# Differential attention of the sample group with the keys along the partitions

## The reference

```python
def diff_attend(q, k, v, q_pos, k_pos, lam, rel_bias):
    s = jnp.einsum('bigrmd,bjgmd->bgrmij', q, k).astype(f32) * (HEAD_DIM ** -0.5)
    dist = q_pos[:, None] - k_pos[None, :]
    bias = rel_bias[rel_bucket(dist)]...            # (tq, tk, 4, 3), the same for both maps
    s = jnp.where(dist >= 0, s + bias, -jnp.inf)
    p = jax.nn.softmax(s, axis=-1)
    a = p[:, :, :, 0] - lam * p[:, :, :, 1]         # the two maps, subtracted
    return jnp.einsum('bgrij,bjgd->bigrd', a, v)    # v has 128 columns
```

## Time and profile before

| | us |
|---|---|
| median of 3 runs | 2465.31 (2454.02 to 2467.85) |
| profiled execution, whole | 2461.47 |
| its span, first to last instruction | 2459.7 |
| PE busy, share of the span | 2230.9 (91%) |
| DVE busy | 1233.1 (50%) |
| ACT busy | 1020.2 (41%) |
| mean granted PE clock | 0.921 |

### The profile page before, as it was taken

The page is one execution under the profiler, slowest core; times in us unless marked ns, Lnnn a source line. Parts: engine busy times, 40 slices in busy tenths (PEclk is TensorE's granted clock), DMA queues, the critical chain, the costliest instruction groups (busy, mean ns, idle before and its releaser), DMA issues. The chain is left out here.

```text
span 2459.7 us, 38651 instructions
## 1 busy us (share of the span) xinstructions
PE 2230.9 (91%) x15123; PEld 1980.8 (81%) x15123; DVE 1233.1 (50%) x2108; ACT 1020.2 (41%) x1569; POOL 416.1 (17%) x396
## 2 busy tenths in 40 slices
PE   6899979999866998999877799699998999979999
PEld 4888869999865456999865466499998888869999
DVE  5666645554442234554446433355546566655554
ACT  3666654443341113443354211444434656644442
POOL 2111102431000002341000000024311111102430
PEclk9899979999986797999985699899999899979999
DMA  5244525658620442657630546056577244436554
GB/s 170 86 134 142 159 70 155 172 156 268 209 76 12 112 125 85 170 160 223 211 103 20 180 139 205 34 162 172 156 238 220 78 142 142 136 94 170 159 154 137
DMA packets 505099, 352.45 MB, mean 143 GB/s; under 512 B 13548, under 2 KB 486398, under 8 KB 504218
## 3 DMA queue, kind: packets, MB, share of 16 engines
q1 hardware_dynamic: 503906, 323.01, 45.3%
q10 hardware_dynamic: 1024, 27.13, 2.8%
HBM read 326.59 MB, written 50.63 MB: 153 GB/s over the span
## 5 line engine op out<-in xcount | busy, mean ns | idle before, releaser
L249 PE MATMUL ps<-xh,wh 128*128 128x288 f32 x2368 | 652.8, 303 | 16.4 <-ACT wh L213 16.2
L221 DVE TENSOR_TENSOR wl<-raw,wh 128x2048 fp32r<-128x2048 f32 (+3 forms) x241 | 501.4, 2082 | 283.7 <-ACT wh L213 282.2
L249 PE MATMUL ps<-xl,wh 128*128 128x288 f32 x2368 | 643.5, 298 | 0.0
L213 ACT ACTIVATE wh<-raw 128x2048 fp32r<-128x2048 f32 (+3 forms) x241 | 419.0, 1741 | 309.9 <-PE ps L257 193.8
L249 PEld LDWEIGHTS ps<-xh,wh 128*128 128x128 f32 x2368 | 452.8, 191 | 18.4 <-issue 14.2
L249 PEld LDWEIGHTS ps<-xl,wh 128*128 128x128 f32 x2368 | 452.4, 191 | 0.5
L257 PE MATMUL ps<-xh,wl 128*128 128x288 f32 x2368 | 353.3, 300 | 0.0
L257 PEld LDWEIGHTS ps<-xh,wl 128*128 128x128 f32 x2368 | 327.0, 190 | 2.3
L473 POOL TENSOR_TENSOR gh<-sg,ut 128x288 f32<-128x288 f32 x88 | 216.6, 2462 | 351.6 <-ACT sg L411 351.6
L249 PE MATMUL ps<-hh,wh 128*128 128x288 f32 x704 | 194.5, 300 | 12.9 <-issue 12.5
L249 PE MATMUL ps<-hl,wh 128*128 128x288 f32 x704 | 193.3, 300 | 0.0
(11 more groups left out here) (317 smaller groups left out, 3113.9 us busy)
## 6 DMA issues: line engine op xcount, KB each, us to landing
raw<-in_ffn_w_in SPq DMA_DIRECT2D x176, 512.0 KB, 5.1
raw<-in_ssm_w_in SPq DMA_DIRECT2D x80, 512.0 KB, 4.9
raw<-in_ffn_w_out SPq DMA_DIRECT2D x64, 384.0 KB, 5.1
raw<-in_ffn_w_out SPq DMA_DIRECT2D x64, 320.0 KB, 3.4
H<-in_state_ssm SPq DMA_DIRECT2D x32, 512.0 KB, 7.4
out_ssm_sample<-H SPq DMA_DIRECT2D x32, 512.0 KB, 6.3
raw<-in_ssm_w_out SPq DMA_DIRECT2D x32, 512.0 KB, 5.3
Kp<-in_cache_diff_k SPq DMA_DIRECT2D x64, 256.0 KB, 4.1
```

Source lines behind the costliest of these rows:

```text
L213: act.activation(wts["hi"][:, s, 0:width], raw[:, s, 0:width], ACT.Copy).then_inc(hi_ready.sem, 1)
L221: dve.tensor_tensor(wts["lo"][:, s, 0:width], raw[:, s, 0:width], wts["hi"][:, s, 0:width].bitcast(F32), ALU.subtract).then_inc(lo_ready.s ...
L249: pe.matmul(out, W[0][:, kk, j, :], x_[:, k, :], stop=False, start=(part == 0 and kk == 0 and x_ is seg.hi), skip_group_check=True)
```

## The change

The sample phase is written anew. Keys now lie along the partitions of the scores:

- `scores` has the turned keys stationary (eight blocks of 128 x 128 per head group) and the 24 queries of the head group moving, and one more matmul for the new tokens. A batch's scores are nine blocks of 96 columns in banks 4 and 5.
- The bias is made in the same shape: 32 matmuls with 33 x 128 blocks of `oh` stationary and `rb` (12 columns) moving, and 4 for the new tokens; 16 DVE copies spread it over the two maps.
- The maximum of a score column now runs over partitions: DVE reduces the nine blocks (`column_max`), PE turns the result (`turn_max`), DVE reduces and puts it on a diagonal (`turn_back`), PE spreads it with a matmul by ones (`spread_max`), DVE subtracts (`shift`), ACT takes the exponential, DVE sums the blocks (`column_sum`), PE spreads the sum (`spread_sum`).
- `values` has the values stationary (128 x 128) and the 24 columns of unnormalised probabilities of both maps moving. DVE divides by the sum, multiplies by lambda and adds the maps into `OT`. There is no turning of probabilities or output, and no copy to `PT`.
- The loops over batches are written out on every engine, and POOL's copy of the queries is gone. SP's loads are as before, with the same two events to wait for.

PE's order in one batch: keys 0, `turn_max` of b-1, keys 1, scores 0, `spread_max` of b-1, keys 2, scores 1, keys 3, scores 2, scores 3, `spread_sum` of b-1, values of b-1.

```diff
             @block.tensor
             def _(pe):
...
-                    for half in range(2):
-                        pe.matmul(ps[32 * g:32 * g + 32, 4 + half, :], Qst[:, r, g, :],
-                                  KT[:, g, half * 512:half * 512 + 512], start=True, stop=True,
-                                  tile_position=(0, 32 * g))
...
+                    for j in range(NPAGES):
+                        bank, o = place(j)
+                        o += 24 * g
+                        pe.matmul(ps[:, bank, o:o + 24], KT[:, g, j * P:(j + 1) * P], Qall[:, b, g, :],
+                                  start=True, stop=True, skip_group_check=True)
+                    o = 288 + 24 * g
+                    mm = pe.matmul(ps[0:NS, 5, o:o + 24], X[:, QD_C + g, SEQ:TOK], Qall[:, b, g, :],
+                                   start=True, stop=True, skip_group_check=True)
...
+                def turn_max(b):
+                    pe.wait_ge(col_max.sem, col_max.at(b + 1))
+                    if b >= 1:
+                        pe.wait_ge(inverted.sem, inverted.at(b))
+                    pe.transpose(ps[0:96, 6, 0:P], cmax[:, b % 2, :], ident).then_inc(max_turned.sem, max_turned.inc())
+
+                def spread_max(b):
+                    pe.wait_ge(max_diag.sem, max_diag.at(b + 1))
+                    pe.matmul(ps[:, 6, P:P + 96], ones[0:96, :], dmax[:, b % 2, :], start=True, stop=True).then_inc(
+                        max_spread.sem, max_spread.inc())
+
+                def spread_sum(b):
+                    pe.wait_ge(col_sum.sem, col_sum.at(b + 1))
+                    pe.matmul(ps[:, 6, P + 96:P + 192], ones, csum[:, b % 2, :], start=True, stop=True).then_inc(
+                        sum_spread.sem, sum_spread.inc())
...
-                            v = Vp[:, r, n, g * P:(g + 1) * P] if n < NPAGES else KV[0:NS, 2, 1, g * P:(g + 1) * P]
-
-                            k, o = (P if n < NPAGES else NS), W * n + g * REP * T
-                            mm = pe.matmul(ps[32 * g:32 * g + 32, 7, 0:P], PT[0:k, r, o:o + 32], v,
-                                           start=(n == 0), stop=(n == NPAGES), tile_position=(0, 32 * g))
...
+                        out, c = ps[:, 7, 24 * g:24 * g + 24], slice(24 * g, 24 * g + 24)
+                        for j in range(NPAGES):
+                            pe.matmul(out, Vp[:, r, j, g * P:(g + 1) * P], Pe[:, j, c],
+                                      start=(j == 0), stop=False, skip_group_check=True)
+                        mm = pe.matmul(out, KV[0:NS, 2, 1, g * P:(g + 1) * P], Pe[0:NS, NPAGES, c],
+                                       start=False, stop=True, skip_group_check=True)
...
+                for j in range(NPAGES):
+                    for t in range(T):
+                        o = NH * (T * j + t)
+                        pe.matmul(ps[:, 4, o:o + NH], oh[:, t, j * P:(j + 1) * P], rb[:, :],
+                                  start=True, stop=True, skip_group_check=True)
...
+                for b in range(NB + 1):
+                    if b < NB:
+                        turn_keys(b, 0)
+                    if b >= 1:
+                        turn_max(b - 1)
+                    if b < NB:
+                        turn_keys(b, 1)
+                        scores(b, 0)
+                    if b >= 1:
+                        spread_max(b - 1)
+                    if b < NB:
+                        turn_keys(b, 2)
+                        scores(b, 1)
+                        turn_keys(b, 3)
+                        scores(b, 2)
+                        scores(b, 3)
+                    if b >= 1:
+                        spread_sum(b - 1)
+                        values(b - 1)
...
             @block.scalar
             def _(act):
...
+                for b in range(NB + 1):
+                    if b < NB:
+                        for g in range(3):
+                            keys(b, g)
+                    if b >= 1:
+                        exps(b - 1)
+                    if b < NB:
+                        keys(b, 3)
...
             @block.vector
             def _(dve):
...
+                for b in range(NB + 1):
+                    if b < NB:
+                        keys(b, 0)
+                    if b >= 1:
+                        turn_back(b - 1)
+                    if b < NB:
+                        keys(b, 1)
+                    if b >= 1:
+                        shift(b - 1)
+                    if b < NB:
+                        keys(b, 2)
+                        keys(b, 3)
+                    if b >= 1:
+                        column_sum(b - 1)
+                    if b < NB:
+                        add_bias(b)
+                        column_max(b)
+                    if b >= 1:
+                        out(b - 1)
```

More of the change, by code:

```diff
@@ L2442, in _ @@
             def _(pool):
[L2443 to L2453, removed]
+                pool.memset(Qall[:, :, :, :], 0.0).then_inc(filled.sem, filled.inc())
@@ L2455, in _, with place @@
+                pool.memset(Sb[:, :, NPAGES, :], NEG).then_inc(filled.sem, filled.inc())
+            def place(j):
+                return (4, 96 * j) if j < 5 else (5, 96 * (j - 5))
             @block.tensor
             def _(pe):
[L2457 to L2462, removed]
@@ L2502, in turn_out @@
-                def turn_out(b, r):
-                    pe.wait_ge(out_staged.sem, out_staged.at(b + 1))
-                    pe.transpose(ps[:, 7, P:2 * P], OS[:, r, :], ident).then_inc(out_turned.sem, out_turned.inc())
[L2506 to L2510, removed]
-                    turn_keys(b, r, 1)
-                    pe.wait_ge(q_staged.sem, q_staged.at(b + 1))
-                    pe.wait_ge(sc_ready.sem, sc_ready.at(3 * b))
-                    scores(b, r, 0)
-                    turn_keys(b, r, 2)
-                    scores(b, r, 1)
-                    if back:
-                        turn_probs(b - 1, 1 - r)
-                    turn_keys(b, r, 3)
-                    scores(b, r, 2)
-                    scores(b, r, 3)
-                    pe.wait_ge(pt_moved.sem, pt_moved.at(2 * b))
-                    for g in range(KVH):
-                        mm = pe.matmul(ps[32 * g:32 * g + 32, 6, NEWC:NEWC + NS], Qst[:, r, g, :],
-                                       X[:, QD_C + g, SEQ:TOK], start=True, stop=True, tile_position=(0, 32 * g))
-                    mm.then_inc(old_scored.sem, old_scored.inc())
-                    if back:
-                        values(b - 1, 1 - r, half - (1 - r))
@@ new lines, in _ @@
+                pe.wait_ge(row_set.sem, row_set.at(1))
+                pe.wait_ge(loaded.sem, loaded.at(2))
+                pe.wait_ge(new_laid.sem, new_laid.at(1))
+                for j in range(NPAGES):
[3 more added lines that the diff above has]
+                                  start=True, stop=True, skip_group_check=True)
+                for t in range(T):
+                    mm = pe.matmul(ps[0:NS, 5, NH * t:NH * t + NH], ohn[:, t, :], rb[:, :],
+                                   start=True, stop=True, skip_group_check=True)
```

292 lines of the change are left out of this document (146 added, 146 removed).

## The result

The changed kernel took 2553.64 us (median of 4 runs, 2546.91 to 2555.73) against 2459.66 for the kernel before in the same job (4 runs, 2454.01 to 2467.85): a ratio of 1.0364, with a 95% interval of 1.0317 to 1.0411, and a difference of 94.0 us. The profiled execution took 2546.91 us, 85.4 more than the profiled one of before.

A forecast was written before the change was run, and what follows sets the result against it. The stage was taken as TensorE's alone: 8 x 30.2 + 2 x 8.7 + 5 + 0.9 = 265 us, less 175.5 and 2.4, gives +87 on 2465.3, 2552 us. Range 2530 to 2585.

The forecast's parts named there:

- points 1, 2 and 4: TensorE per full-clock batch: scores 7.2 us against 7.0, values 8.6 against 8.8, together 20.9 (20.4 to 21.7) against 20.42.
- The draw: By instruction times alone the change neither gains nor loses: 20.9 us a batch against 20.42.
- The clock: Narrow matmuls lower TensorE's clock, transposes raise it: per batch 3.8 us low, 9.9 full, 16.5 low, together 30.2.
- A missed batch: A batch whose transposes miss the clock's rise stays low throughout: 38.9 us.
- How many batches miss: Two of eight batches let miss the clock's rise, 8.7 us for each.
- rival C: Mixed scores and transposes lose the full clock, or more batches miss: +105 to +125 us, about 2580; chance 0.16.
- point 5: VectorE's reductions, 1.0 us each in 9 us of work, hide under TensorE's batch of at least 20: cost nothing.
- point 6: Preparation: bias matmuls 14.7 us against 15.5, key transposes no longer wait for table copies; keys start 2.4 us earlier (0 to 4).
- point 7: Last batch's softmax steps follow each other while TensorE waits: 5 us (4 to 6), then values and 0.9 us of scaling.
- Rival A: Gapless narrow matmuls hold the full clock through the stage: -5 us (-8 to +5), 2460 us; chance 0.12.
- Rival B: The clock never comes back within the stage: +139 us, 2604 us; chance 0.04.

The follow-up runs named there:

- wide72_inorder: Changed kernel in its own order, tail and loads, every score and value matmul 72 columns wide for 24, scores laid out group by group: 2480.42 us, stage 223.3.
- after_again: The changed kernel itself, unedited, run again in the other job on another chip: 2570.01 us, ratio 1.0424, stage 304.9.
- wide_all: Changed kernel with scores 96, 72, 48 and 72 columns, values 96, scores 3 between value groups 1 and 2, sums spread later: 2480.48 us, stage 216.8.
- wide_tail: wide_all plus a second buffer of probabilities and another order in the last batch: 2466.31 us, ratio 1.0011, stage 206.7.
- keys_together: Changed kernel, all widths still 24, the four key transpose groups in a row at the head of each batch: 2572.46 us in one run, stage 306.1.
- values96: Changed kernel with value matmuls of 96 columns for 24, scores left at 24: 2551.02 us, ratio 1.0315, stage 304.1.
- wide72: wide_tail with every score and value matmul 72 columns wide and scores laid out group by group: 2483.30 us, ratio 1.0089, stage 211.6.
- wide72_early: wide72 with the one-hot table, bias row and page table loaded during the prompt part: 2470.00 us, ratio 1.0046, stage 202.6.
- wide_inter: Changed kernel with scores 96, 72, 48 and 24 columns, values 96, scores 3 between value groups 1 and 2: 2502.38 us, stage 240.3.
- scores_wide: Changed kernel with scores of 96, 72, 48 and 24 columns alone, values still 24 and order unchanged: 2551.54 us in one run, stage 278.4.

## Why the prediction was right

It said 2552 us; the runs gave 2553.6 and, in the other job, 2570.0. The mechanism is the forecast one, but the 1.6 us between 2552 and 2553.6 are luck in part. The forecast is 2465.3 + 87. The change cost 94.0 us between the medians (90.2 in the profiled stage, 106.6 between the medians of the other job), and the median of the kernel before came out at 2459.7 with its fourth run, which made up for it. Point by point:

- **Scores and values (points 1, 2 and 4).** Scores: 0.113 forecast, 0.112 measured. Values: 0.2145 forecast at the low clock, 0.221 measured, and the pair 0.55 for 0.6; a group 4.09 us for 4.03. The full-clock batch of 20.9 us never occurs in after; wide72_inorder's is 21.98 with 72 columns, and taking off the 0.05 us by which each of its eight groups of 16 is slower and the 0.07 for each of four pairs of new keys, and nothing for the pairs on 32 rows, leaves an estimate of 21.3, inside the 20.4 to 21.7. The draw would have been a loss of about 0.9 us a batch.
- **The clock.** Low under keys 0 and 1, full for about 10 us, low under the values: right, and the batch is 30.4 us for 30.2. The rise was put under the transposes, 3.3 to 3.5 us after their beginning; it came 3.5 to 4.6 us after (4.3 in batch 0, by the 0.89 over 1393 to 1395 for transposes from 1389.12), all but once a little into scores 0. A missed batch: 38.9 forecast, 39.1 measured.
- **How many batches miss.** Two of eight was the one number that rested on no row, and it is the term that was mis-sized: two in one execution, in the other three and most of batch 0, at 8.7 us (5.4 for batch 0). That is all of the 13.8 us between the two stages, and nearly half of what separates the profiled executions. The forecast put this into rival C and the range, which both medians are inside. The misses don't look like mere chance: in batches 4 to 7 of after the rise comes 3.5, 3.8, 4.1 and 4.4 us after the transposes begin, and in batches 3 to 6 of after_again 3.8, 4.1, 4.5 and 4.8. It slips 0.3 us later from batch to batch, and the batch after one of 4.6 (batch 3 of after) or 4.8 (batch 7 of after_again) misses it. Why it does, no run shows.
- **VectorE (point 5).** The strided reductions were priced at 1.0 us and took 1.6. The prediction priced TensorE's waits for them within a batch at nothing and named such a wait as a sign of being wrong. There is one, of 1.5 us in the first full batch (1.0 in after_again), and none in the six others:

```profile
L2633 DVE TENSOR_REDUCE cmax<-Sb 128x96 f32<-128x864 f32 x8 | 12.9, 1615 | 0.3
L2656 DVE TENSOR_REDUCE csum<-Pe 128x96 f32<-128x864 f32 x8 | 12.9, 1612 | 1.0 <-ACT Pe L2563 1.0
L2490 PE MATMUL ps<-cst,cmax 128*96 128x128 f32 x8 | 3.4, 428 | 1.5 <-DVE cmax L2633 1.5
L2499 PE MATMUL ps<-csum,cst 128*128 128x96 f32 x16 | 4.9, 399 | 3.7 <-DVE csum L2656 3.7
```

(These are groups of after over the stage: busy us, mean ns, idle before and its releaser.)

- **Preparation (point 6).** 64 bias matmuls took 13.73 us, 0.214 each, for 0.213; the keys begin 21.0 us after the prompt part, 2.9 us sooner than before, for 2.4.
- **Tail (point 7).** 5 us forecast, 6.3 measured from 1634.46 to 1640.76, of which TensorE waits 4.6 and its small instructions are the rest. The reduction at its end took 1.6 us for the forecast 1.0. The last values took 16.3 us at the low clock, for 16.5 in the sum; it had fallen at 1618.7 already, under the values of the batch before. Where it had held that far, as in wide_all, the tail's waits let it fall: wide_tail, which mends both, has a stage 10 us shorter.
- **Rival A** (busy without a gap keeps the clock) fails by 261.65 us busy of 268.62 at 0.61. The Trainium skill (TensorE: Matmul & The Clock Gate, Why this matters for your kernels) warns of idle gaps between bursts alone; this trace disagrees, since the clock fell with none. That section of the Trainium skill also advises padding a thin M, against the throughput that waits for DMA between bursts cost. No run here tests that: what wide72_inorder widened is the columns that stream, and it gave back 68 us where the batches had no such waits.
- **Rival B** (no rise at all) fails in after and more plainly in keys_together. The Trainium skill (TensorE: Matmul & The Clock Gate, Part 4: PE-mode transpose) has transposes not count for the full clock. The trace of keys_together disagrees: all eight rises came while transposes ran, 3.8 to 7.2 us after the first of them, with nothing but transposes since the narrow matmuls before. In after most rises came up to 1.0 us into scores 0.

## What to carry to other kernels

Making the large operand stationary and streaming a narrow one can cost nothing by instruction times (0.112 us an instruction against 0.115 for three times the columns) and still lose half of TensorE's speed: a row of such matmuls fills the engine and lets its clock fall. Look at the granted clock beside the busy time, and before reordering anything, widen the streams with whatever columns lie beside, up to where they stop hiding behind the load (here 72 columns held the clock in the batches and 96 in the tail too); here every narrow stretch had to go, for a single one left in a batch still took the clock away in four of seven full batches. And compare stages cut at the same points, since a clock that is gained or missed elsewhere moves the whole by more than a small edit does.

## What the runs showed of the hardware

- Behind a load of 128 columns each of the two instructions of an f32 matmul takes 0.112 us for 24 columns, 0.113 for 48 (1.81 us for 16), 0.115 for 72 and 0.121 for 96; at the low clock 0.221 for 24 and 0.229 for 96 (3.66 us for 16, values96).
- Six batches in a row at 72 columns held the full clock (wide72_inorder), but it fell 11.9 and 13.1 us into the longer row of value groups of 72 columns in the tails of wide72 and wide72_early, where 96 columns held it (wide_tail). It fell after 3.8 us of 24 columns in a row (values96), and after 2.1 us of them between 96-column groups in four of seven batches (wide_inter). Among wide matmuls it fell in or within 0.6 us after a wait of 1.9 to 2.0 us in four of five kernels (wide_all, wide_tail, wide72 and wide72_inorder, not wide72_early). With scores of 96, 72 and 48 columns and narrow values the clock held for about 10 us a batch and fell within the first values (scores_wide).
- 96-column matmuls in an unbroken row at the low clock did not raise it in 17 us (values96), where transposes of 128 columns did within 2.5 us behind them (1630.38 for transposes from 1627.90) and within 3.5 to 7.2 us elsewhere (keys_together). What makes the difference is not settled. Nor is width all: the 24 bias instructions of the kernel before, 16 of them 512 columns wide over 33 partitions, kept TensorE busy for 15.5 us, and the clock stayed at 0.50 throughout (1379.76 to 1395.27).
- VectorE's reduction of 864 elements a row to 96, nine to each, 96 apart, takes 1.61 us, where one over 1056 side by side took 1.25; a reciprocal of 96 elements a row from PSUM takes 0.75 us, three times as long as a product of the same size, one operand of it from PSUM as well (0.26).
